# Per-chunk waits in the output products of a feed-forward block

## The reference

```
def swiglu(h, w_in, w_out):
    gate, up = jnp.split(h @ w_in, 2, axis=-1)
    return (jax.nn.silu(gate) * up) @ w_out

x = x + g2 * swiglu(rms_norm(x, norm_ffn[i]) * (1.0 + sc2) + sh2, ffn_w_in[i], ffn_w_out[i])
```

## Time and profile before

| | |
|---|---|
| median of 3 runs | 3079.18 us (3075.61 to 3079.61) |
| profiled execution, its own time | 3078.68 us |
| its span, first to last instruction | 3076.9 us |
| PE busy | 2785.1 us, 91% of the span |
| DVE, ACT, POOL busy | 1012.7, 1083.7, 913.7 us |
| mean granted clock of TensorE | 0.941 of full speed |

### The profile page before, as it was taken

The page is one execution under the profiler, slowest core; times in us unless marked ns, Lnnn a source line. Parts: engine busy times, 40 slices in busy tenths (PEclk is TensorE's granted clock), DMA queues, the critical chain, the costliest instruction groups (busy, mean ns, idle before and its releaser), DMA issues.

```text
span 3076.9 us, 42170 instructions
## 1 busy us (share of the span) xinstructions
PE 2785.1 (91%) x16424; PEld 2244.7 (73%) x16424; DVE 1012.7 (33%) x1758; ACT 1083.7 (35%) x1846; POOL 913.7 (30%) x418
## 2 busy tenths in 40 slices
PE   6899999767679589899999998999979998999999
PEld 4788888665655378688888875778756665777877
DVE  3655520365767400211111114221335653021111
ACT  3343331436366220421111214332445555242221
POOL 2122232443445352222222212222200004344443
PEclk8999999878789799899999998999989998999999
DMA  6344443203020241011121113343352221222222
GB/s 243 126 150 155 153 156 124 108 22 113 22 83 15 76 138 67 31 65 64 60 67 57 51 46 127 130 148 113 103 184 62 62 62 38 85 73 93 94 96 83
DMA packets 111033, 288.26 MB, mean 94 GB/s; under 512 B 9904, under 2 KB 41136, under 8 KB 104624
## 3 DMA queue, kind: packets, MB, share of 16 engines
q1 hardware_dynamic: 95920, 265.91, 25.5%
q10 hardware_dynamic: 14976, 20.45, 1.8%
HBM read 239.27 MB, written 47.05 MB: 93 GB/s over the span
## 4 chain that ended last, share of the span: by engine, by line
PE 81%; DVE 7%; ACT 4%; issue 3%; POOL 2%; DMA 2%; SPq 0%; POOLq 0%; DVEq 0%; ACTq 0%
PE ps L503 19%; PE ps L504 19%; PE ps L505 18%; PE ps L1169 3%; PE ps L1145 3%; PE ps L1157 2%; PE ps L1135 1%; PE ps L1074 1%; PE ps L880 1%; DVE ps L2190 1%; DVE Vall L2194 1%; PE ps L577 1%; PE ps L1045 1%; PE ps L1046 1%; PE ps L1047 1%
## 5 line engine op out<-in xcount | busy, mean ns | idle before, releaser
L485 POOL TENSOR_TENSOR Wl<-raws,Wh 128x2048 fp32r<-128x2048 f32 (+3 forms) x140 | 599.5, 4283 | 1722.3 <-ACT Wh L479 1722.3
L503 PE MATMUL ps<-Hh,Wh 128*128 128x512 f32 x2144 | 763.5, 356 | 33.2 <-DVE Hl L2049 15.8
L504 PE MATMUL ps<-Hl,Wh 128*128 128x512 f32 x2144 | 756.0, 353 | 0.0
L505 PE MATMUL ps<-Hh,Wl 128*128 128x512 f32 x2144 | 750.5, 350 | 0.0
L503 PEld LDWEIGHTS ps<-Hh,Wh 128*128 128x128 f32 x2144 | 408.6, 191 | 114.4 <-issue 37.1
L505 PEld LDWEIGHTS ps<-Hh,Wl 128*128 128x128 f32 x2144 | 407.4, 190 | 57.3
L504 PEld LDWEIGHTS ps<-Hl,Wh 128*128 128x128 f32 x2144 | 408.9, 191 | 51.3
L479 ACT ACTIVATE Wh<-raws 128x2048 fp32r<-128x2048 f32 (+3 forms) x140 | 247.5, 1768 | 457.1 <-PE ps L505 425.5
L2398 DVE SCALAR_TENSOR_TENSOR xT<-ps,mod,xT 128x512 f32 x96 | 60.6, 659 | 520.7 <-PE ps L505 520.7
L503 PE MATMUL ps<-Gh,Wh 128*128 128x512 f32 (+1 forms) x528 | 191.7, 363 | 17.6 <-DVE Gl L2418 17.6
L2415 DVE TENSOR_TENSOR hdb<-sgb,ps 128x768 f32<-128x768 f32 (+1 forms) x44 | 36.1, 821 | 500.0 <-PE ps L505 500.0
(11 more groups left out here) (341 smaller groups left out, 4486.9 us busy)
## 6 DMA issues: line engine op xcount, KB each, us to landing
raws<-in_slabs SPq DMA_DIRECT2D x234, 512.0 KB, 4.5
ada<-in_ada SPq DMA_DIRECT2D x32, 1024.0 KB, 5.1
adb<-in_ada SPq DMA_DIRECT2D x16, 1024.0 KB, 5.6
chunks<-obuf ACTq DMA_DIRECT2D x52, 256.0 KB, 2.0
chunks<-obuf ACTq DMA_DIRECT2D x52, 128.0 KB, 1.9
chunks<-ebuf SPq DMA_DIRECT2D x17, 384.0 KB, 2.6
mst<-mix SPq DMA_DIRECT2D x16, 384.0 KB, 5.0
raws<-in_slabs SPq DMA_DIRECT2D x16, 384.0 KB, 3.8
```

The costliest lines, as they stand in the source:

```text
L485: nc.gpsimd.tensor_tensor(Wl[n % 2][:, 0:w], raw[n % 2][:, 0:w], Wh[n % 2][:, 0:w].bitcast(f32), ALU.subtract).then_inc(sig("slab_lo"), 1)
L503: nc.tensor.matmul(o, lhs(c)[0], rhs(c, t0, t1)[0], start=(s == 0), stop=False)
L504: nc.tensor.matmul(o, lhs(c)[0], rhs(c, t0, t1)[1], start=False, stop=False)
L505: last = nc.tensor.matmul(o, lhs(c)[1], rhs(c, t0, t1)[0], start=False, stop=(s == k - 1))
```

## The change

Before, PE waited ahead of the output products of a group until all hidden chunks of the group were written, high and low. Now it waits ahead of each inner chunk for the low part of that chunk alone. `ready` is called only in the first product of each of the two passes.

```diff
         def pe_ffn(pe, layer, w):
             for grp, n in enumerate(GROUPS):
                 pe_wide(pe, f"fi{layer}{grp}", KD, Hh, Hl, w, ready=None if grp else normed(pe, 2 * layer + 1))
-                pe.wait_ge(sig("hid_lo"), 22 * layer + sum(GROUPS[:grp + 1]))
-                pe.wait_ge(sig("hid_hi"), 22 * layer + sum(GROUPS[:grp + 1]))
-                pe_wide(pe, f"fo{layer}{grp}", n, Gh, Gl, w)
+                first = 22 * layer + sum(GROUPS[:grp])
+                pe_wide(pe, f"fo{layer}{grp}", n, Gh, Gl, w, ready=lambda s: pe.wait_ge(sig("hid_lo"), first + s + 1))
```

## The result

The changed kernel takes 3047.62 us (median of 4 runs, 3046.74 to 3049.02), the kernel before on the same chip 3079.39 us (4 runs). The ratio is 0.9898 with a 95% interval of 0.9884 to 0.9911: faster by 1.0%, 31.8 us. The forecast was 3051 us, a gain of 28.1 us. The profiled execution took 3046.74 us, its span is 3045.0 us.

The account below looks back on a forecast made before the run. PE sets the time, stopping at six group starts for `Gl`. Standing 17.6 us, lower clock 9.4 and remaining 1.1 make 28.1 us; 3078.68 less 28.1 gives 3050.6, forecast as 3051 us, range 3045 to 3058.

Parts of the forecast that it names:

- The stops: PE's waits for `Gl` ahead of the six groups' output products, 17.6 us in all, taken as all gone.
- the late chunk: Last chunk of each group: earlier chunks' work hides its making, 0.9 us to spare in layer 1's group 2.
- The clock: Behind four of six stops PE ran at the lower clock, 9.4 us together; taken as returned with the stops.
- The split: At the six group starts, 28.1 us: 17.6 standing still, 9.4 at half rate, 1.1 remaining.
- standing: PE standing still for `Gl` at the group starts: 9.9 us in layer 0, 7.7 in layer 1, 17.6 in all.
- the low stretches: Work at the lower clock behind four stops, terms 1.7, 3.0, 3.0 and 1.7, together 9.4 us.
- the restart: Remaining 1.1 us at the six stops, some 0.2 each, put down to restart and cut-off ends of slow stretches.
- The 76 more waits: In the output products 88 chunk waits replace 12 group waits; met waits were taken to cost zero.
- What is late next: Weight slab for a pass's second half, tightest in layer 1's group 2: comes 1.6 us early, cost nothing.

Follow-up runs that it names:

- late_second: The changed kernel with the late chunk taken second in the output products' order of inner chunks; 3063.48 us, ratio 0.9948 to the kernel before.
- filled_stop: The kernel before, group-wide waits kept, with matmuls of unused results put into each of the six stops; 3065.95 us, ratio 0.9965.
- undo_layer0: The changed kernel with the group-wide waits restored in layer 0 alone; 3066.82 us, ratio 0.9961 to the kernel before.
- undo_layer1: The changed kernel with the group-wide waits restored in layer 1 alone; 3060.75 us, ratio 0.9939 to the kernel before.
- before_again: The kernel before, unchanged, run again; 3077.72 us, ratio 0.9999.
- after_again: The changed kernel, unchanged, run again; 3045.54 us, ratio 0.9899 to the kernel before.
- more_waits: The changed kernel with four identical waits ahead of every chunk of every output product, 1408 instead of 88; 3049.19 us, ratio 0.9910 to the kernel before.
- two_waits: The changed kernel with only two waits in each product that carries waits, 24 instead of 88; 3048.38 us, ratio 0.9904 to the kernel before.
- filled_short: The changed kernel with 5, 5 and 3 calls of unused matmuls in PE's idle time at three block entries; 3048.38 us, ratio 0.9904 to the kernel before.
- filled_entries: The changed kernel with 22, 22 and 15 calls of unused matmuls in PE's idle time at three block entries; 3050.9 us, ratio 0.9912 to the kernel before.

## Why the prediction was right

The direction, the size and the mechanism held; the time lies in the range and 3.4 us under the value.

- *The stops.* All six are gone and the late chunk is covered with 0.9 us to spare at the tightest place; late_second shows that the cover is the work ahead of it.
- *The clock.* Its loss was returned with the stops. filled_stop shows that this part exists by itself, and undo_layer0 and undo_layer1 that it comes back with them. The prediction took it from one execution, where four of six stops drew it; in before_again and the two undo kernels all of the stops did. The group starts of the kernel before then cost 29.6 us, and those of the two undo kernels together 29.5. So this term was sized some 1.5 us too small by reading a single profile. The prediction also says that nowhere else in the products' stretches did the clock fall. That isn't so at the entry: the kernel before was granted 0.63 from 1262 to 1270 us, as the changed one is 0.59 from 1263 to 1271. These stretches are in both kernels, so the sum doesn't change.
- *The split.* The on-record working gave standing 17.6 us, the low stretches 9.4 and the restart 1.1. The measured one is 19.5 us for the late start, restart included, and 8.6 us for the clock in that same execution. So the restart is (19.5 - 17.6) / 6 = 0.3 us for each stop, not 0.2, with 0.06 of it there even without a stop. The 9.4 us are a little large for one reason that the trace shows: the working put 6.0 us for the third stop because its row repeats the second's, but that row covers only 5.6 us, which makes its term 2.8 and the sum 9.2:

```profile
1780.40:1786.00 5.60, 5.58 (x17) 0.50 0.21 31
```

- *The 76 more waits.* Taken as zero, and zero they are, up to 16 times as many.
- *What is late next.* Nothing, as forecast; the slab is 1.6 us early.
- *The remainder.* Of the difference between the two first profiles 4.1 us lie outside the group starts. The stretch between the two blocks lies behind layer 0's group starts and ahead of layer 1's waits, so what can act on it is whether layer 0 has its stops. With them it took 956.4 to 957.5 us (before 957.5, before_again 956.8, filled_stop 956.6, undo_layer0 956.7, late_second 956.4; mean 956.8), without them 954.5 to 959.0 us (after 954.5, after_again 955.6, more_waits 956.1, two_waits 956.9, undo_layer1 959.0; mean 956.4). The two sets overlap, and the first profile of the changed kernel is the lowest of all, so these profiles give no sign that the 3.0 us belong to the change. The 1.1 us ahead of the first group start are small beside chance too: there the ten profiles hold the same program, and the last `hdb` of the first group starts anywhere from 1391.1 to 1397.3 us. No run was made to settle an effect of under a microsecond or so.

## What to carry to other kernels

Where a consumer waits for a whole group and only the last part is late, wait part by part and take the late part last; the gain is the whole stop as long as the work ahead of the late part is longer than the chain that makes it (here 3.4 us against 2.5 at the tightest). Price a stop of TensorE by when the next result comes, not by the idle time alone: here 17.6 us of idle time cost 28 to 30. Keeping the clock up paid here where TensorE set the pace (filled_stop, 11.2 us); where its input was late, the faster clock only made it wait longer (filled_short, nothing).

## What the runs showed of the hardware that was not expected

- Behind stops of 3.3 us (layer 0) the granted clock fell in 9 of 9 cases (before, before_again, undo_layer0); behind stops of 2.6 us (layer 1) in 7 of 9 (before, before_again, undo_layer1); behind stops of 2.1 and 1.7 us in none of 6 (late_second). The length of one stop doesn't decide alone: at layer 0's entry in filled_short, where PE waits again and again, the clock stayed at 1.00 behind one wait of 2.07 us (1261.1 to 1263.6) and was 0.50 soon behind another of 2.07 us (1266.7 to 1269.3). Where it fell behind the first stop of a profile, one execution of the same kernel had a granted clock of 0.63 over 4.6 us and another 0.54 over 6.5 us.
- With the stops the same program scattered from 3070.9 to 3086.2 us over ten runs; the changed kernel's eight runs lie between 3044.3 and 3049.7 us. That the stops cause the wider scatter was not tested by itself, and filled_entries, which doesn't have them either, ran from 3048.4 to 3061.1 us.
- A product with 32 met waits in it takes 8.41 us, as one without.
- A filling matmul of `ones` with `sqb` (plain 32-bit operands) shows as two instructions: 22 calls gave 44 in 19.1 us, 0.43 us each at a granted clock of 1.00, while one of `Hh` with `Hh` took 3.14 us for 13, 0.24 us each.
